# A hybrid attention step: index scores of the two head halves into two banks, index steps moved beside their query chunks, gate units in pairs

## The reference, cut to what matters

```python
mod = silu(c) @ w_ada + b_ada; shift, scale, gate = split(mod, 3)
h = rmsnorm(x, ln_gain) * (1 + scale) + shift
proj = h @ w_in          # q_a, ckv, krope, g_a, q_b, k_b, v_b, q_i, k_i, w_i, g_b
# head group A: latent attention -> o_a
# head group B: an indexer chooses keys, then attention over them
dots  = einsum('btge,bse->btgs', q_i, k_i) * 64 ** -0.5    # 16 index heads of width 64
score = einsum('btgs,btg->bts', relu(dots), w_i)           # masked by chunks of 64
sel   = top_k(score, k)                                    # 64 keys of 256, 36 keys of 144
o_b   = softmax(q_b @ k_sel + rel_bias) @ v_sel
y = concat(rmsnorm(o_a) * silu(g_a), rmsnorm(o_b) * silu(g_b))
out = rmsnorm(x + gate * (y @ w_out)) * final_gain         # and new cache rows are returned
```

## Time and profile before

| | us |
|---|---|
| median of 3 runs | 982.42 (981.59 to 984.57) |
| the profiled execution | 981.87 |
| its span in the trace | 980.1 |
| TensorE matmul busy | 923.8 (94%) |
| DVE / ACT / POOL busy | 431.9 / 332.5 / 116.6 |

### The profile page before, as it was taken

How to read it: one execution, slowest core, us unless ns; L and a number is a source line. 1 busy time by engine, 2 the same in 40 slices (tenths; PEclk the granted TensorE clock), 3 DMA queues, 4 the chain that set the end, 5 groups by cost and what they waited for, 6 DMA issues and landing times.

```text
span 980.1 us, 14093 instructions
## 1 busy us (share of the span) xinstructions
PE 923.8 (94%) x5661; PEld 789.3 (81%) x5661; DVE 431.9 (44%) x871; ACT 332.5 (34%) x610; POOL 116.6 (12%) x187
## 2 busy tenths in 40 slices
PE   4799899999999999999999999999979999979996
PEld 1367588899998688888999888787868898868885
DVE  3432343436332144433332553368235566666462
ACT  2222243333311234223321532333224345633341
POOL 1000012102100000020113000011011103540000
PEclk9799999999999999999999999999999999999999
DMA  9999968765533234464334676447666742783423
GB/s 335 384 382 382 379 191 258 171 156 159 139 121 95 68 91 133 140 181 155 114 105 139 219 245 213 153 133 215 213 219 202 241 165 87 284 268 108 129 65 128
DMA packets 129554, 185.37 MB, mean 189 GB/s; under 512 B 30065, under 2 KB 79913, under 8 KB 128337
## 3 DMA queue, kind: packets, MB, share of 16 engines
q1 hardware_dynamic: 116176, 141.85, 45.6%
q0 software_dynamic: 13312, 42.61, 13.2%
HBM read 173.84 MB, written 12.69 MB: 190 GB/s over the span
## 4 chain that ended last, share of the span: by engine, by line
PE 73%; DMA 6%; DVE 4%; ACT 2%; issue 2%; POOL 2%; SPq 0%; DVEq 0%; ACTq 0%; POOLq 0%
PE proj L1761 28%; PE proj L1750 24%; DMA gl_b<-gate_scratch 2%; PE proj L1777 2%; PE bankO L1872 1%; PE bankO L1881 1%; PE proj L1734 1%; DMA kload<-in_cache_dsa_k 1%; PE bankS L1777 1%; DMA raw<-in_w_in 1%; PE bankS L1998 1%; PE bankT L2013 1%; PE bankS L1949 1%; DVE w_lo L1271 1%; PE bankO L1975 1%
## 5 line engine op out<-in xcount | busy, mean ns | idle before, releaser
L1271 DVE TENSOR_TENSOR w_lo<-raw,w_hi 128x1024 fp32r<-128x1024 f32 (+2 forms) x164 | 198.5, 1217 | 230.6 <-ACT w_hi L934 229.8
L934 ACT ACTIVATE w_hi<-raw 128x1024 fp32r<-128x1024 f32 (+2 forms) x164 | 167.3, 1026 | 191.1 <-PE proj L1750 102.6
L1761 PE MATMUL proj<-hT_hi,w_hi 128*128 128x384 f32 x608 | 212.3, 349 | 3.5 <-DVE w_lo L1271 2.3
L1761 PE MATMUL proj<-hT_hi,w_lo 128*128 128x384 f32 x608 | 204.1, 336 | 0.0
L1761 PE MATMUL proj<-hT_lo,w_hi 128*128 128x384 f32 x608 | 203.9, 335 | 0.0
L1750 PE MATMUL proj<-w_hi,hT_hi 128*128 128x512 f32 (+2 forms) x464 | 180.5, 389 | 7.5 <-POOL hT_lo L873 4.9
L1750 PE MATMUL proj<-w_hi,hT_lo 128*128 128x512 f32 (+2 forms) x464 | 175.0, 377 | 0.0
L1750 PE MATMUL proj<-w_lo,hT_hi 128*128 128x512 f32 (+2 forms) x464 | 174.9, 377 | 0.0
L1761 PEld LDWEIGHTS proj<-hT_hi,w_hi 128*128 128x128 f32 x608 | 114.5, 188 | 15.7 <-issue 10.5
L1761 PEld LDWEIGHTS proj<-hT_lo,w_hi 128*128 128x128 f32 x608 | 114.6, 188 | 0.5 <-issue 0.2
L1761 PEld LDWEIGHTS proj<-hT_hi,w_lo 128*128 128x128 f32 x608 | 114.4, 188 | 0.0
(11 more groups left out here) (366 smaller groups left out, 1076.5 us busy)
## 6 DMA issues: line engine op xcount, KB each, us to landing
raw<-in_w_in SPq DMA_DIRECT2D x104, 512.0 KB, 3.8
araw<-in_w_ada SPq DMA_DIRECT2D x128, 256.0 KB, 8.8
raw<-in_w_ada SPq DMA_DIRECT2D x32, 512.0 KB, 4.5
raw<-in_w_out SPq DMA_DIRECT2D x32, 512.0 KB, 3.8
raw<-in_w_in SPq DMA_DIRECT2D x32, 256.0 KB, 3.2
raw<-in_w_in SPq DMA_DIRECT2D x32, 128.0 KB, 2.8
wuk<-in_w_uk POOLq DMA_DIRECT2D x16, 256.0 KB, 3.7
kload<-in_cache_dsa_k POOLq DMA_DIRECT2D x8, 512.0 KB, 5.7
```

The costliest lines, as they stand in the source:

```text
L934: return nc.scalar.activation(out, in_, func, scale=scale, **kw)
L1271: V.tensor_tensor(w_lo[:, SLOT[u], 0:w], raw_of(u)[:, 0:w], high(u)[:, 0:w].bitcast(F32), ALU.subtract).then_inc(lo_ready, 1)
L1761: ins = mm(banks[blk][:, 0:TOK], w[:, n, cols], a[:, kt, :], start=first and n == m == 0, stop=final and n == per - 1 and m == 2)
```

## The change

1. *Two banks.* `ip` and `is` compute heads of both halves in turn, those of the even heads into bank S and those of the odd heads into bank T. The semaphore between the halves of `is` is gone. `rl` becomes two buffers. There are 6 steps `ip` in place of 12, with twice the heads each.
2. *Moved prompt steps.* `ip` 0 to 3 stand two rows behind the query chunk that they need (rows 159, 167, 169 and 175), and wait for that chunk's eviction. `ip` 4 and 5 stand in rows 190 and 191. `is(0)` moves from row 183 to 182, where the last `qi` unit is now in row 181.
3. *Rows of the rounds.* `tk` takes every second row from 190 to 204. `ld_mask` moves from row 196 to 205 and `comb` from 198 to 208.
4. *Gates in pairs.* Two gate units follow each two dense units.
5. *Stores and loads.* The eight stores of the modulation rows move to row 227 (`st_gate`), and the loads of gates 12 to 15 from rows 235 and 236 to row 234.

```diff
-        if CHUNKS[u[0]][0] in ("qi", "qb"):
-            out.append(gate.pop(0))
+        if CHUNKS[u[0]][0] in ("qi", "qb") and u[1] % 2:
+            out += [gate.pop(0), gate.pop(0)]
...
-    "kic": "T", "ip": "S", "is": "T", "iacc": "O", ...
+    "kic": "T", "ip": "ST", "is": "ST", "iacc": "O", ...
...
+    for n, v in enumerate((LAST_UNIT["qi", 0] + 2, LAST_UNIT["qi", 1] + 2, LAST_UNIT["qi", 1] + 4,
+                           LAST_UNIT["qi", 2] + 2, u + 8, u + 9)):
+        put(v, ("ip", n))
...
-    for n in range(len(ROUNDS)):
-        put(u + n, ("tk", n))
-    put(u + 5, ("ld_mask", 0))
-    put(u + 7, ("comb", 0))
+    run(u, "tk", len(ROUNDS), 2)
+    put(u + 2 * len(ROUNDS) - 1, ("ld_mask", 0))
+    put(u + 2 * len(ROUNDS) + 2, ("comb", 0))
...
+    put(u + 3, ("st_gate", 0), ("st_gate", 1))
...
-        put(max(u, v - 3), ("ld_g", 8 + i))
+        put(u, ("ld_g", 8 + i))
...
+INDEX_PARTS = [(1, 0, 2, 0), (1, 4, 2, 1), (0, 0, 4, 1), (1, 8, 2, 2), (1, 12, 2, 3), (0, 8, 4, 3)]
...
         def ip(n):                                   # ACT
-            filled(act, "ip", n, "S")
             if n:
                 act.wait_ge(sem("ip_sum"), n)
-            nc.scalar.activation(rl[:], bank["S"][:], ACT.Relu).then_inc(free["S"], 1)
+            for a, b in enumerate("ST"):
+                filled(act, "ip", n, b)
+                nc.scalar.activation(rl[a][:], bank[b][:], ACT.Relu).then_inc(free[b], 1)
...
         def ip(n):                                   # TensorE
-            out = take("ip", n, "S")
+            t, g0, per, chunk = INDEX_PARTS[n]
+            moved(pe, "qi", chunk)
+            outs = [take("ip", n, b) for b in "ST"]
+            w = SEQ if t else P
+            for q in range(per):
+                for a, b in enumerate("ST"):
+                    r = slice(IE * a, IE * (a + 1))
+                    ins = mm(outs[a][:, w * q:w * (q + 1)], q_iT[r, g0 // 2 + q, P * t:P * (t + 1)], kiT[r, 0:w],
+                             start=True, stop=True)
+                    if q == per - 1:
+                        ins.then_inc(full[b], 1)
...
         def is_(b):                                  # TensorE
-                if a:
-
-                    ins.then_inc(sem("is_even"), 1)
-                    pe.wait_ge(sem("is_even"), b + 1)
-                ins = mm(out[:, NKEY * a:NKEY * (a + 1)], q_isT[r, b].rearrange("p h t -> p (h t)"), kicT[r, b, :],
-                         start=True, stop=True)
-            ins.then_inc(full["T"], 1)
+                mm(outs[a][:, 0:NKEY], q_isT[r, b].rearrange("p h t -> p (h t)"), kicT[r, b, :],
+                   start=True, stop=True).then_inc(full[name], 1)
```

More of the change, by code:

```diff
@@ L297, in plan @@
         if i < 8:
-            put(u + i, ("ip", i), ("is", i))
-    for i in range(8, 12):
-        put(u + i, ("ip", i))
+            put(u + i, ("is", i))
     u += 8
-    for n in range(len(ROUNDS)):
-        put(u + n, ("tk", n))
-    put(u + 5, ("ld_mask", 0))
-    put(u + 7, ("comb", 0))
+    run(u, "tk", len(ROUNDS), 2)
+    put(u + 2 * len(ROUNDS) - 1, ("ld_mask", 0))
+    put(u + 2 * len(ROUNDS) + 2, ("comb", 0))
     put(u - 7, ("ld_k", 0), ("ld_k", 1))
@@ L309, in plan @@
     put(u + 4, ("kl", 2))
-    u = max(u + len(ROUNDS), LAST_UNIT["qb", 3] + 1)
+    u = max(u + 2 * len(ROUNDS) + 3, LAST_UNIT["gate", 1])
     put(u - 1, ("ld_kc", 0))
@@ L874, in yh, with st_gate @@
                                     ALU.subtract).then_inc(sem("hT_ready"), 1)
+        def st_gate(j):
+            moved(pool, "gate", j)
+            for g in range(4):
+                c0 = 1024 * j + 256 * g
+                pool.dma_start(gate_d[:, c0:c0 + 256], modA[32 * g:32 * g + 9, j, :]).then_inc(gate_out, 16)
         def ld_gate(_):
@@ L906, in _ @@
                                    stage[:, 0:2, 0:TOK]).then_inc(staged_out, 16)
[L907 to L911, removed]
             for name, n in PLAN[u]:
@@ L1169, in ip @@
         def ip(n):
[L1170 removed]
             if n:
                 act.wait_ge(sem("ip_sum"), n)
[L1173 removed]
+            for a, b in enumerate("ST"):
+                filled(act, "ip", n, b)
+                nc.scalar.activation(rl[a][:], bank[b][:], ACT.Relu).then_inc(free[b], 1)
         def is_(b):
[L1176 removed]
             if b:
                 act.wait_ge(sem("iacc_pe"), b)
[L1179 to L1180 removed]
+            for a, name in enumerate("ST"):
+                filled(act, "is", b, name)
+                nc.scalar.activation(rls[:, a, :], bank[name][:, 0:NKEY], ACT.Relu).then_inc(free[name], 1)
         def kl(t):
@@ L1551, in ip @@
                 link(V.tensor_copy(idx[:, 1, :], negmask[:, P:3 * P]))
[L1552 to L1559, removed]
+            t, g0, per, _ = INDEX_PARTS[n]
+            w = SEQ if t else P
+            for a, b in enumerate("ST"):
+                emptied(dve, "ip", n, b)
+                for q in range(per):
+                    g = g0 + a + 2 * q
+                    ins = V.scalar_tensor_tensor(out=idx[:, t, 0:w], in0=rl[a][:, w * q:w * (q + 1)],
+                                                 scalar=wis[:, t, g:g + 1], in1=idx[:, t, 0:w],
+                                                 op0=ALU.mult, op1=ALU.add)
+                    if a == 0 or q < per - 1:
+                        link(ins)
             ins.then_inc(sem("ip_sum"), 1)
@@ L1990, in ip @@
         def ip(n):
-            out = take("ip", n, "S")
[L1992 to L2000, removed]
+            t, g0, per, chunk = INDEX_PARTS[n]
+            moved(pe, "qi", chunk)
+            outs = [take("ip", n, b) for b in "ST"]
+            w = SEQ if t else P
+            for q in range(per):
+                for a, b in enumerate("ST"):
+                    r = slice(IE * a, IE * (a + 1))
[3 more added lines that the diff above has]
+                        ins.then_inc(full[b], 1)
         def is_(b):
-            out = take("is", b, "T")
+            moved(pe, "qi", 3)
+            outs = [take("is", b, name) for name in "ST"]
             if b == 0:
@@ L2020, in iacc @@
                 pe.wait_ge(sem("wsel_ready"), 1)
-            pe.wait_ge(free["T"], USES["is", b, "T"] + 1)
+            for name in "ST":
+                pe.wait_ge(free[name], USES["is", b, name] + 1)
             for a in range(2):
```

12 lines of the change are left out of this document (4 added, 8 removed), and 2 rows, old and new, of the table STEP_BANKS.

## The result

The changed kernel takes 960.90 us (median of 4 runs, 958.61 to 962.68). The kernel before, on the same chip, takes 982.32 (981.59 to 984.57). The ratio is 0.9764 with a 95% interval of 0.9745 to 0.9784. The forecast was 957.6, its own range 953 to 962, so the time fell inside, 3.3 us above the forecast. The profiled execution is the slowest of the four (962.68, span 960.9).

A forecast was written before the change was run, and what follows sets the result against it. TensorE, busy 94% of the span, was taken as the bound. Terms -4.1 - 8.5 - 2.3 - 5.6 - 7.8 + 3.5 = -24.8 from 981.87 gave 957.1, plus 0.55 for the median: 957.6 us, range 953 to 962.

The forecast's parts named there:

- gates in pairs: Gate units among dense units: 11 fewer excursions out of the dense matmuls at 0.37 us each, 4.1 us less.
- two banks: Index steps `ip` and `is`: the two array halves run beside each other, 8.5 us less.
- rounds on every second row: Top-k rounds on DVE: spread over twice the rows, TensorE's two waits for `w_lo` go, 2.3 us less.
- stores out of the keys' way: Second load of cached keys no longer behind four stores: TensorE's wait and half clock go, 5.6 us less.
- gates 12 to 15 early: First output chunks: earlier gate loads remove TensorE's 4.90 us wait and the half clock behind it, 7.8 us less.
- added waits, foreseen: New TensorE waits at `ip`, `is`, `kl(0)` and `ds(0)`, with too little in front: 3.5 us more, between 1 and 8.
- the four short covers: Four places with only a gate unit between a sample step and what reads it: 0.8 us of added waits in all.
- rival 5: Dense unit behind each pair waits for a late `w_lo` split, 1.7 us for each of 16 pairs: 985; chance 0.04.
- Rival 1: After the late gates, something hidden behind them comes next, giving back up to 7.8 us: 965.4; chance 0.12.
- nothing that I can see: End of the kernel: nothing visible is late after the gates, as the weights had all landed by then.
- Rival 3: Index steps: matmuls go in program order, each step one matmul longer, 2.1 us in all: 959.7; chance 0.10.
- Rivals 2: Index steps: the array halves do not overlap when they alternate, price 7.2 us: 964.8; chance 0.08.

The follow-up runs named there:

- the halves apart: Changed kernel, but in each `ip` and `is` step all of bank S first, and TensorE waits until it is full before bank T; 969.26 us.
- ldg_back: Changed kernel with the loads of gates 12 to 15 back in their later rows, behind the residual and modulation loads; 967.66 us.
- stores_back: Changed kernel with the eight stores of the modulation rows back behind the last gate unit of each half; 964.95 us.
- gates_single_wsel: Changed kernel with the `wsel` step three rows later and one gate unit behind each dense unit again; 962.25 us.
- halves_in_turn: Changed kernel with each prompt step doing all even-half matmuls into bank S, then all odd-half ones into bank T, without a wait between; 961.17 us.
- wsel_later: Changed kernel with the step that fills `wsel` on DVE three rows later, row 156 in place of 153; 956.79 us.

## Why the prediction was right, and where 3 us went

The direction and the main terms held.

| step of the sum | forecast | measured |
|---|---|---|
| gates in pairs | -4.1 | -4.1 start to start; 5.5 and 7.5 when undone, with waits that single gates add |
| two banks | -8.5 | -8.4 start to start (23.5 to 15.1); 9.3 with the halves apart |
| rounds on every second row | -2.3 | 1.5 when undone, not told from 0; 2.1 in the trace |
| stores out of the keys' way | -5.6 | 5.0 when undone |
| gates 12 to 15 early | -7.8 | 7.7 when undone |
| added waits, foreseen | +3.5 | +2.0 |
| `w_lo` behind the `wsel` step | none | +3.7 where the clock fell behind it, else +2.1 |

With the last two lines (2.0 + 3.7) in place of the 3.5, and the other terms as forecast, the sum is -22.6: 981.87 - 22.6 + 0.55 = 959.8. The two medians are 960.9 and 959.96.

- **Added waits.** The term was mis-sized in both directions. The foreseen ones were smaller: `ip` 0, 1 and 3 waited 0.13 each (0.2 forecast), `is(0)` 0.57 with nothing on top of the 0.61 of before (0.5 forecast), the four short covers 0.26 and 3 x 0.14, `kl(0)` 1.69 against the 1.43 of before, `ds(0)` 0.70 more. That is 0.4 + 0.7 + 0.3 + 0.7 = 2.0 with the small gain of `is(0)`. The missing one is 2.09 us of wait and 1.6 of slow clock. The wait is in all seven profiles that have this order and the `wsel` step in row 153; behind it the clock fell to 0.50 in five of them and stayed at 1.00 in two (`ldg_back`, `stores_back`).
- **The step that failed** is the sentence in rival 5. It priced a late split as something behind every pair, and judged it by DVE's idle time over the whole kernel (230 us). DVE had the time in all pairs but one, the dense units of rows 156 and 157. There a dense unit moved (to row 153) ahead of the step behind which DVE waits 3.25 us for POOL and works 2.34 on `wsel`. That split was 2.2 us early before, and the order brings its reader 4.4 us nearer. An average said nothing of this row.
- **Rounds.** The term took two waits away; undone beside the pairs, they come back in another place (`kl(1)`) and smaller. The waits of 1.04 and 1.22 us thus belonged to single gates and dense rounds together: `gates_single_wsel`, with single gates and the rounds spread, has no wait for `w_lo` there either.
- **Rival 1** (the end gives it back) is there in small. In every profile with the gates early an output weight block is 3.8 to 5.6 us late for ACT. In five of them TensorE waits 0.2 to 1.9 us behind it; in the others it does not wait. Of the 7.8 us next to nothing was lost: undoing it costs 7.7. But the prediction's "nothing that I can see" rested on the transfers' share of 0.08 behind the wait. From 848.6 to 873.5 of the same trace, ahead of the wait, the share was about 1.0, so that window did not tell how late the weights would be once TensorE came earlier.
- **Rival 3** (program order) did not happen in the alternating order, since bank T starts with bank S. The Trainium skill, "TensorE: Matmul & The Clock Gate", on packing small matmuls, has matmuls in strict program order. The traces of `halves_in_turn` do not agree: a bank T matmul started 0.01 us after the first of four bank S ones that stand ahead of it.
- **Rivals 2 and 5** are out: the halves apart cost 9.3 us, and no dense unit from 553 us to `ks(0)` has a wait for `w_lo`, so late splits behind each pair did not come.

## What to carry to other kernels

When units are regrouped, look at each row that they move through for what the helper engines do there. The slack of each split against its reader decides, not an engine's mean idle time. A wait of some 2 us on a full TensorE can cost almost twice its length (2.09 and 1.6 here), since the clock may fall behind it, so the short waits that a change adds are worth a second edit: here three of them gave back 7.9 us of 960. Two products that use half of the rows each are worth issuing in turn into two banks; it halved their time.

## What was not expected of the hardware

- TensorE lets a matmul of the free half of its rows pass earlier ones of the busy half, but not any number: in `halves_in_turn`, behind four of them bank T started 0.01 us after bank S, behind eight it started 0.55 us after, at bank S's fifth matmul.
- The same wait has no fixed price. The one of 1.69 us at `kl(0)` is in six profiles of almost the same program: in five the granted clock stayed at 1.00 behind it, in one (`wsel_later`) it was 0.50 for some 3.2 us. The one of 2.09 us at `w_lo` is in seven, and the clock fell to 0.50 behind it in five. The four of 3.4 us and more that are shown here were each followed by 0.50.
